# A transformer block with 32 experts on one core: the experts' weights through one ring of five buffers, eight units in the early sweep, and the end in quarters

## What is computed

```python
ada = silu(c) @ w_ada + b_ada                 # six vectors of 2048
h = rms_norm(x, g_pre_mix) * (1 + sc_m) + sh_m
y = token_mixer(h, ...)                       # h @ w_in (2048 x 6160), attention beside a gated scan, @ w_out
x = x + gt_m * rms_norm(y, g_post_mix)
h = rms_norm(x, g_pre_ffn) * (1 + sc_f) + sh_f
y = hier_moe(h, ...)                          # 32 experts, each row goes to two of one group
x = x + gt_f * rms_norm(y, g_post_ffn)
# an expert: (silu(t @ w1) * (t @ w3) * weight) @ w2, with w1, w3: 2048 x 512 and w2: 512 x 2048
```

## Time and profile before

| | us |
|---|---|
| median of 3 runs | 1546.67 (1545.41 to 1547.28) |
| the profiled execution, its own time | 1547.03 |
| its span, first to last instruction | 1545.2 |
| PE matmuls busy | 1168.6 (76%) |
| DVE busy | 717.6 (46%) |
| HBM read | 579.28 MB, 376 GB/s over the span |
| chain that ended last | PE 46%, DMA 35%, DVE 8% |

### The profile page before, as it was taken

The page is one execution under the profiler, slowest core; times in us unless marked ns, Lnnn a source line. Parts: engine busy times, 40 slices in busy tenths (PEclk is TensorE's granted clock), DMA queues, the critical chain, the costliest instruction groups (busy, mean ns, idle before and its releaser), DMA issues.

```text
span 1545.2 us, 21972 instructions
## 1 busy us (share of the span) xinstructions
PE 1168.6 (76%) x9147; PEld 602.4 (39%) x9148; DVE 717.6 (46%) x939; ACT 168.8 (11%) x432; POOL 41.1 (3%) x69
## 2 busy tenths in 40 slices
PE   5679999999999998757647646656655679699554
PEld 4568644754444454323223223222322334344221
DVE  5773256777484635422422422432332345446326
ACT  3001131221111020000000000000000000001001
POOL 0002000000000001000000000000000000000001
PEclk9789999999999997978877877887887889899877
DMA  9999877778788788999999999999999998999994
GB/s 360 395 401 358 318 301 300 299 274 342 269 306 332 300 331 339 429 426 425 434 424 425 432 426 425 434 423 425 431 426 425 431 427 372 387 389 391 427 426 180
DMA packets 93822, 581.83 MB, mean 377 GB/s; under 512 B 5752, under 2 KB 16272, under 8 KB 55904
## 3 DMA queue, kind: packets, MB, share of 16 engines
q1 hardware_dynamic: 91056, 571.49, 90.8%
q10 hardware_dynamic: 1520, 7.76, 1.2%
q0 software_dynamic: 1216, 2.17, 0.5%
HBM read 579.28 MB, written 2.13 MB: 376 GB/s over the span
## 4 chain that ended last, share of the span: by engine, by line
PE 46%; DMA 35%; DVE 8%; issue 5%; SPq 4%; ACT 1%; POOL 0%; DVEq 0%; ACTq 0%
DMA stream<-in_w 32%; PE ps L803 12%; PE ps L638 11%; PE ps L722 7%; PE ps L829 5%; DMA stream<-in_w_ada 3%; PE ps L555 3%; PE ps L635 3%; SPq L435 3%; PE ps L773 2%; DVE wk L1201 1%; DVE wk L876 1%; DVE wk L1195 1%; SPq L495 1%; DVE stream L925 1%
## 5 line engine op out<-in xcount | busy, mean ns | idle before, releaser
L803 PE MATMUL ps<-stream,wk 128*32 128x256 f32 x4608 | 310.4, 437 | 271.3 <-DMA stream<-in_w 269.8
L1153 DVE TENSOR_TENSOR acc<-ps,acc 128x2048 f32<-128x2048 f32 x37 | 84.8, 2292 | 576.7 <-PE ps L773 576.7
L803 PEld LDWEIGHTS ps<-stream,wk 128*32 128x32 f32 x4608 | 177.9, 126 | 417.1 <-issue 349.7
L638 PE MATMUL ps<-stream 128*128 128x512 f32 x448 | 197.3, 595 | 0.0
L829 PE MATMUL ps<-stream,wk 128*32 128x512 f32 x1152 | 131.2, 595 | 18.0 <-DVE wk L1205 18.0
L638 PEld LDWEIGHTS ps<-stream 128*128 128x128 f32 x448 | 83.5, 191 | 98.9 <-issue 98.8
L722 PE MATMUL ps<-stream 128*128 128x512 f32 x256 | 112.3, 601 | 3.1 <-ACT stream L1384 1.8
L555 PE MATMUL ps<-stream 128*128 128x256 f32 x448 | 107.0, 404 | 1.8 <-ACT stream L1280 1.8
L555 PEld LDWEIGHTS ps<-stream 128*128 128x128 f32 x448 | 91.3, 205 | 15.6 <-issue 1.9
L773 PE MATMUL ps<-wk,cst 32*128 32x512 f32 x592 | 84.1, 639 | 11.1 <-DVE acc L1153 10.1
L876 DVE SCALAR_TENSOR_TENSOR wk<-stream,cc,wk 128x1024 f32<-128x1024 f32 (+1 forms) x75 | 80.4, 1072 | 13.1 <-DMA stream<-in_w_ada 9.5
(11 more groups left out here) (247 smaller groups left out, 825.0 us busy)
## 6 DMA issues: line engine op xcount, KB each, us to landing
stream<-in_w SPq DMA_DIRECT2D x128, 2048.0 KB, 24.6
stream<-in_w SPq DMA_DIRECT2D x32, 4096.0 KB, 32.4
stream<-in_w_ada SPq DMA_DIRECT2D x64, 1024.0 KB, 5.6
stream<-in_w_ada SPq DMA_DIRECT2D x64, 512.0 KB, 11.7
stream<-in_w_in SPq DMA_DIRECT2D x8, 4096.0 KB, 16.7
stream<-in_w_out SPq DMA_DIRECT2D x4, 4096.0 KB, 15.8
stream<-in_w_in SPq DMA_DIRECT2D x3, 3584.0 KB, 18.9
stream<-in_w_in SPq DMA_DIRECT2D x2, 1792.0 KB, 10.7
```

The lines of the kernel that those rows point to most:

```text
L638: last = nc.tensor.matmul(bank(fill % 2), hT[:, k, P * half:P * half + P], w[:, k, :], start=(k == 0), stop=(k == KD - 1))
L803: last = nc.tensor.matmul(bank(1)[32 * g:32 * g + 32, 0:256], xe[:, k, :], a13[g // 2][:, k, 256 * (g % 2):256 * (g % 2) + 256], start=(k ...
L1153: V.tensor_tensor(y4, ps[:, b0:b0 + 4, :], y4, ALU.add).then_inc(ysum_sb, 1)
```

## The change

The three kinds of expert weights go through one ring. Load n (3e for w1 of expert e, 3e+1 for w3, 3e+2 for w2) uses buffer n mod 5, each in two halves with semaphores of their own. SyncE waits for the use of load n-5, which is w3 of e-2, w2 of e-2 or w1 of e-1: so w1 of e waits for the first product of expert e-2, w3 of e for the second product of e-2, w2 of e for the first product of e-1. PE's loop does five experts in a pass, and the last two are written out behind it.

In the early sweep there are eight units of 256 columns. Six keep a bank; units 6 and 7 take turns in one bank, and DVE adds their part of each stage to SBUF (`added`), in the midst of the next stage's pieces. PE takes the units in the order 6, 0, 1, 2, 7, 3, 4, 5. The half unit and its two slots are gone: 32 slots, attention from slot 6.

At the end PE puts the second half's earlier sum into PSUM with an identity product and adds the last part on top, DVE multiplies that with the gain straight from PSUM, ScalarE makes the roots, and both halves are finished and sent in four quarters each.

```diff
+RING = 5
-HEADS_READY = [10, 12]
+HEADS_READY = [8, 10]
-EARLY = 7
-SLOTS = 34
-ATT_FROM = 7
+EARLY = 8
+HELD = 6
+TURN = [6, 0, 1, 2, 7, 3, 4, 5]
+SLOTS = 32
+FILLS = HELD + SLOTS // 2
+ATT_FROM = 6
+ADA_AT = [0, 11, 21, SLOTS, SLOTS + 6]
...
-        early_w = [slab(s4, 4096, 2, 1792), slab(s3, 0, 4, 1792), slab(S2, 0, 4, 1792), slab(s3, 0, 4, 1792), slab(S2, 4096, 2, 1792)]
+        early_w = [slab(S2, 0, 2, 2048), slab(s3, 0, 4, 2048), slab(S2, 0, 4, 2048), slab(s3, 0, 4, 2048), slab(S2, 4096, 2, 2048)]
-        W1 = [stream[:, 0, :], stream[:, 1, :]]
-        W3 = [stream[:, 2, :], stream[:, 3, :]]
-        W2v = stream[:, 4, :].rearrange("p (k n) -> p k n", k=4)
+        def ring(n):
+            return stream[:, (0, 2, 4, 1, 3)[n % RING], :]
@@ SyncE
-                if j >= 3:
+                if j >= 2:
                     sp.wait_ge(stage_ps, j - 1)
                 sp.dma_start(early_w[j], w_in[:, lo:hi, 0:256 * EARLY]).then_inc(early_w_in[j], 16)
-            sp.dma_start(half_w, w_in[:, :, 256 * EARLY:2048]).then_inc(half_in, 16)
...
-            def load_w1(e, b):
+            def load_w1(e, r):
                 done = sp.value_load(cums[0:1, bass.ds(e - 1, 1)], min_val=1, max_val=MAX_TILES)
                 sp.wait_ge(ab_ps, done)
-                sp.dma_start(W1[b], w_unit(e, w1)).then_inc(w1_in[b], 16)
-            def load_w3(e, b):
                 for j in range(2):
-                    sp.dma_start(half(W3[b], j), half(w_unit(e, w3), j)).then_inc(w3_in[b][j], 16)
-            def load_w2(e):
+                    sp.dma_start(half(ring(r), j), half(w_unit(e, w1), j)).then_inc(ring_in[r % RING][j], 16)
+            def load_w3(e, r):
+                done = sp.value_load(cums[0:1, bass.ds(e - 1, 1)], min_val=1, max_val=MAX_TILES)
+                sp.wait_ge(ye_ps, done)
+                for j in range(2):
+                    sp.dma_start(half(ring(r), j), half(w_unit(e, w3), j)).then_inc(ring_in[r % RING][j], 16)
+            def load_w2(e, r):
                 done = sp.value_load(cums[0:1, bass.ds(e, 1)], min_val=1, max_val=MAX_TILES)
-                sp.wait_ge(ye_ps, done)
+                sp.wait_ge(ab_ps, done)
...
-            with sp.Fori(2, NE // 2) as i:
-                for b in range(2):
-                    load_w1(2 * i + b, b)
-                    load_w3(2 * i + b, b)
-                    load_w2(2 * i + b)
+            with sp.Fori(1, NE // RING) as i:
+                for b in range(RING):
+                    load_w1(RING * i + b, 3 * b)
+                    load_w3(RING * i + b, 3 * b + 1)
+                    load_w2(RING * i + b, 3 * b + 2)
@@ PE
             def early_unit(j, u):
                 lo, hi = STAGES[j]
+                held = u < HELD
+                if not held and j + u > HELD:
+                    pe.wait_ge(add_sb, 2 * j + u - HELD)
...
-            with pe.Fori(0, NE // 2) as i:
-                for b in range(2):
+            with pe.Fori(0, NE // RING) as i:
+                for b in range(RING):
+                    expert(i, b)
+            for b in range(NE % RING):
+                expert(NE // RING, b)
...
+            def earlier_sum(g):
+                nc.tensor.matmul(ps[:, g, :], ident, ysum[1][:, 512 * g:512 * g + 512], start=True, stop=False)
+            earlier_sum(0)
+            pe.wait_ge(ye_sb, total + 1)
             add_part(0, 4)
-            add_part(1, 0)
+            for g in range(1, 4):
+                earlier_sum(g)
+            add_part(1, 0, True)
@@ DVE
+            def added(j, u):
+                home = kaT[:, 2 * u - 8:2 * u - 6, :]
+                n = 2 * j + u - HELD
+                dve.wait_ge(add_ps, n + 1)
+                if j == 0:
+                    V.tensor_copy(home, bank(HELD, 2, S)).then_inc(add_sb, 1)
+                else:
+                    dve.wait_ge(add_sb, n)
+                    V.tensor_tensor(home, bank(HELD, 2, S), home, ALU.add).then_inc(add_sb, 1)
...
+                    if j and n_ in (len(pieces(j)) // 4, 3 * len(pieces(j)) // 4):
+                        added(j - 1, HELD + n_ // (len(pieces(j)) // 2))
...
             collect(0, 4)
+            link(V.tensor_tensor(fin_gained(0), ysum[0], g2b, ALU.mult))
-            collect(1, 0)
+            for j in range(2):
+                V.tensor_tensor(fin_gained(1)[:, 1024 * j:1024 * j + 1024]..., ps[:, 2 * j:2 * j + 2, :],
+                                g2b[:, 1024 * j:1024 * j + 1024]..., ALU.mult).then_inc(gain_sb, 1)
@@ ScalarE
-            for t in range(TT):
-                act.wait_ge(fin_sb, t + 1)
-                act.dma_start(out_d[:, t, :], fin_gained(t)).then_inc(fin_out, 16)
+            for t in range(TT):
+                for q in range(4):
+                    act.wait_ge(fin_sb, 4 * t + q + 1)
+                    act.dma_start(out_d[:, t, 512 * q:512 * q + 512], fin_gained(t)[:, 512 * q:512 * q + 512]).then_inc(fin_out, 16)
```

More of the change, by code:

```diff
@@ L124, in schedule @@
     beside = [[] for _ in range(SLOTS)]
[L125 to L129, removed]
+    beside[0].append(("alpha", 0))
+    beside[1].append(("row",))
+    beside[2] += [("alpha", 1), ("lam",)]
+    beside[4].append(("alpha", 2))
+    beside[5].append(("flip",))
     for m in (2, 3):
@@ L162, in loads @@
 def loads():
-    out = [(4 * i + 5.9, ("unit", i + 2)) for i in range(8)] + [(SLOTS + 2 * i + 1.9, ("unit", i + 10)) for i in range(2)]
+    out = [(4 * i + 3.9, ("unit", i + 2)) for i in range(8)] + [(SLOTS + 2 * i + 1.9, ("unit", i + 10)) for i in range(2)]
     out += [(max(ada_slot(n - 4) + 0.5, 1.9), ("ada", n)) for n in range(4, 64)]
@@ L550, in early_unit @@
                 lo, hi = STAGES[j]
+                held = u < HELD
+                if not held and j + u > HELD:
+                    pe.wait_ge(add_sb, 2 * j + u - HELD)
                 for part in range(2):
                     for k in range(lo, hi):
-                        if u == 0 and part == 0:
+                        if u == TURN[0] and part == 0:
                             pe.wait_ge(hT_act, k + 1)
-                        last = nc.tensor.matmul(bank(u, 2, S)[:, part, :], early_w[j][:, k - lo, 256 * u + P * part:256 * u + P * part + P], hT[:, k, :],
-                                                start=(k == 0 and part == 0), stop=(k == KD - 1 and part == 1))
+                        last = nc.tensor.matmul(bank(u if held else HELD, 2, S)[:, part, :], early_w[j][:, k - lo, 256 * u + P * part:256 * u + P * part + P], hT[:, k, :],
+                                                start=(k == (0 if held else lo) and part == 0), stop=(k == (KD if held else hi) - 1 and part == 1))
+                if not held:
+                    last.then_inc(add_ps, 1)
                 return last
@@ L579, in mod_sums @@
                 return last
-            fill = EARLY
+            fill = HELD
             for item in SCHED:
@@ L768, in pick_rows, with add_part @@
                 last.then_inc(rows_ps, 1)
-            def add_part(t2, b0):
+            def add_part(t2, b0, onto=False):
                 for g in range(4):
-                    last = nc.tensor.matmul(ps[:, b0 + g, :], spread[32 * g:32 * g + 32, t2, :], ye[32 * g:32 * g + 32, :], start=True, stop=True)
+                    last = nc.tensor.matmul(ps[:, b0 + g, :], spread[32 * g:32 * g + 32, t2, :], ye[32 * g:32 * g + 32, :], start=not onto, stop=True)
                 last.then_inc(part_ps, 1)
@@ L868, in early @@
                 out_ = early_acc[:, :, P * lo:P * hi]
-                for c, k0, k1 in pieces(j):
+                for n_, (c, k0, k1) in enumerate(pieces(j)):
                     dve.wait_ge(piece_in[c % 8], 32 * (c // 8 + 1))
@@ L910, in _ @@
                 early(j)
+            for u in range(HELD, EARLY):
+                added(len(STAGES) - 1, u)
             def accumulate(n):
```

283 lines of the change are left out of this document (151 added, 132 removed).

## The result

The changed kernel takes **1537.68 us** (median of 4 runs, 1536.35 to 1538.39) where the kernel before took 1546.97 beside it (1545.41 to 1548.34). The ratio is 0.994, with a 95% interval of 0.9926 to 0.9954: faster by 9.3 us. The prediction had 1524.7 us, with bounds that it works out as 1518.6 and 1533.8, so its direction was right and its size was not: it had named a gain of 22.3 us. The profiled span fell from 1545.2 to 1534.5 us.

The account below looks back on a forecast made before the run. The prediction took PE work to bound the first third and the weights' bytes the expert part. Savings of 15.6 (experts), 3.7 (sweep) and 3.0 (end), together 22.3, from 1547.03 gave 1524.7 us; range 1518.6 to 1533.8.

Parts of the forecast that it names:

- the experts' sum of -15.6 us: Expert part: the ring removes 14.3 us lost at two pairs and 1.3 us of emptiness at the start.
- their fetch: Rival, expert loop: five bodies do not stay resident and each expert's code is fetched again, 1567 us; chance 3%.
- Sweep: Early sweep: an eighth unit replaces two later slots; 3.3 + 1.5 + 5.6 - 14.05 = -3.7 us.
- term (1): Early sweep: 1.31 MB more goes ahead of stage 3's last modulation piece, costing +3.3 us.
- term (3): Early sweep: 24 records of the new unit fall into PE-bound work at 0.2335 us each, costing +5.6 us.
- the rival in which PE and DVE wait for each other: Early stages give back their gain, with a doubled attention stall: sweep +2 instead of -3.7, 1530 us; chance 12%.
- Start of the experts: Loads of the first experts: the ring issues w2 of expert 1 earlier, removing 1.3 us of emptiness.
- Experts 3 to 23: Steady expert stretch: the bytes stay the same, at 29.44 us an expert, so no change.
- The two pairs: Experts 23, 24, 26 and 27 with two tiles of rows: the ring loses nothing there, saving 14.3 us.
- slack of 5.6 us: At the pairs: the buffer comes free 5.6 us before the load needs it, some 1.3 us going to starting a transfer.
- End: Kernel's end: -1.2 us of DVE work and -1.8 for a smaller last transfer, -3.0 us; bounds -1 and -4.5.
- The third, the blocks: Sign against the forecast: a fetch row of more than some 60 blocks with PE idle beside landed weights.

Follow-up runs that it names:

- ten halves: The changed kernel's sweep and end, PE loop of three experts with two written out ahead, ten half buffers in a fixed table of places; 1526.68 us.
- loop of eight: The kernel before with only PE's expert loop written out eight times instead of two; 1563.34 us against 1547.87.
- loop of two: The changed kernel with PE's loop of two experts, w1 loaded whole and fixed uses for the ten half buffers; 1533.57 us.
- loop of four: The kernel before with only PE's expert loop written out four times instead of two; 1556.91 us, ratio 1.0065.
- ring alone: The kernel before with the change's ring and loop of five experts, without its sweep and end; 1543.24 us, ratio 0.9976.
- nine halves with two experts ahead: The changed kernel with a ring of nine half buffers, experts 0 and 1 written out ahead of a loop of three; 1531.52 us.
- w1 in halves: The kernel before with each w1 loaded as two halves in rows of 16 KB; 1550.48 us, ratio 1.0018.
- kernel without the ring: The changed kernel with its sweep and end, but experts, buffers and PE's loop of two as before; 1542.34 us, ratio 0.9968.

## Why the prediction was wrong

**The failed step is the experts' sum of -15.6 us** (measured, by the terms below, -1.9), and in it the price of code, which was put at nothing. The prediction took 29.44 us an expert as fixed by the bytes and asked of the loop of five only whether PE stalls longer than its 10.3 to 11.1 us of waiting. It saw that no row told whether five bodies stay resident, and put 3% on their fetch; for stalls at the five jumps back alone it took nothing. What happened is neither of the cases it priced. The bodies are fetched again in every expert (40 blocks in twenty experts, 2 x 16 KB for a body of some 26 KB), PE has its waits for weights to hide it in, and the *load queue* pays: 7.5 us over twenty experts after the short rows are taken out (597.9 less 590.4 of the ten halves), 0.19 us a block, beside 0.17 and 0.16 in the two kernels with written-out loops, with 36 and 19 blocks.

These prices are averages, and the cost is not spread evenly. Fifteen of the change's twenty experts take 29.40 to 29.72 us with 1 to 3 blocks each; the other five take 30.83 to 30.98 with 2 or 3 blocks, and they hold 7 of the 7.5 us. In the loop of eight, eight of the twenty take 30.1 to 30.2 us and the others 29.4 to 29.6.

In the case where fetching was priced as slower than before, PE had to stall. The trace of the change has a stop of 5.80 us before expert 25, where the loop jumps back, with one block on its way in it; it lies behind the twenty quiet experts in which the 7.5 us were lost. The stops before experts 2 and 29 (2.86 and 3.25 us) have no block in them, and the loop of two waits 2.81 us before expert 2 for its weights, so these two are not shown to be fetches.

That the blocks are the cause is shown: with them and without the ring it is slower, with the ring and without them it is fast. The loop of four shows it within one run. How one block of 16 KB delays the weights by 0.16 to 0.19 us, when 16 KB at 427 GB/s are 0.04 us, is argued, with three readings for it. The argument: a block occupies one of the 16 DMA engines, that engine falls behind the others, and PE waits for the part of a load that it carries. First, q8's 0.4% of 16 engines over 860 us is 1.0 us of one engine's time a block. Second, twenty experts need 251.7 MB, and the kernels without blocks move 251.5 to 251.7 MB between the starts of experts 3 and 23; the change moves 253.2 and the ring alone 253.3, the loops of eight and four 252.8 and 252.2. So 1.6 MB more had come in, worth 3.7 us, while the load that PE needed was not complete. Third, when the queue runs low at the pairs, the DMA share falls to nothing within 3 us in the kernel before (0.77, 0.19, 0.04, 0.00 in the windows of 1 us from 1283), and in the change it is 0.81, 0.57 and 0.54 in the three from 1279 and 0.85, 0.62 and 0.38 in the three from 1312, when SyncE's next load is issued: some engines have work left when others have none. No experiment here was made on it, and why some blocks cost nothing stays open.

Term by term, by the table (spans; forecast, measured):

- *Sweep:* -3.7, measured **-5.3** in this execution. The fold of stage 3 was worked out to come at 120.5 and came at 120.60, but that is luck. DVE's new wait was put at nothing, and 1.98 of its 26.9 us lie on the path to this fold; the late start of the pieces, term (1), was 2.1 us in place of 3.3 (96.26 against 94.12), the two additions took 1.2 in place of 1.5, and the 14 pieces 0.4 less than before. In the nine halves with two experts ahead the same wait is 0.54 us, and the fold comes 1.4 us earlier, at 119.21. From fold to fold PE's loop took 33.45 us, where 32.4 were worked out. The error that shows in the sum is in term (3): the 224 records behind the fold take 50.75 us to the first slot, 0.227 each, where 0.2335 were used. So the rival in which PE and DVE wait for each other had its mechanism right, at 2 us once, and not its sum.
- *Start of the experts:* -1.3, measured **-0.3**. The hole in the queue is filled (423 GB/s from 615 to 620, where 313 were), but PE's wait before expert 2 only fell from 3.37 to 2.86 us. It is 2.87 in the ten halves and 2.81 in the loop of two. What sets it is not shown.
- *Experts 3 to 23:* 0, measured **+9.1**: 1.5 for rows of 16 KB (from w1 in halves: 0.074 x 20) and 7.5 for blocks. Here the forecast fails.
- *The two pairs:* -14.3, measured **-10.7**. The difference of 3.6 is as large as 8 x 0.45 us of the slower pace. But the reasoning with a slack of 5.6 us did not hold as written: the queue ran low ahead of w2's issues at 1281.69, 1314.66 and 1405.98, the first of which, behind expert 23, the prediction had not looked at. What this cost by itself is not shown: the queue was never wholly empty, the 1.6 MB that had come in ahead were used up in this stretch (99.3 MB moved where eight experts need 100.7), and expert 29 starts 179.5 us after expert 23, six times the pace again. The run with ten halves has nearly the full size, -13.5, with a table made to give the loads at the pairs their place earlier. Whether five whole buffers would do it without blocks no run shows. The nine halves show the price of a ring that is too short: 6.5 us more than with ten.
- *End:* -3.0, measured **-3.4**.

The sum is -10.6 against a measured span of -10.7. The early stages did not give back their gain. Of what the prediction said would show it wrong, two came: windows under 400 GB/s at the pairs (283 to 341), and DVE's new wait in the early stages, 26.9 us where more than 3 was the sign. The second was a poor sign, as most of that wait cost nothing. The third, the blocks, came at 55 in the window, below the 60 that it had named and with PE mostly waiting for weights rather than beside them: the sign that mattered was set too high.

The rule that the prediction set against the change, from the Trainium skill, Runtime: NRT & Kernel Launch, Instruction fetch mechanics, gives PE 128 KiB, and lets a jump stall when its target is outside "the current 2-page window", with pages of 16 KiB. The prediction read the whole buffer as that window, and the runs bear it out in so far as two bodies (53 KB by the prediction's estimate) and three (80 KB) jump back without a block. They agree that a limit exists but not quite with its place: four bodies (107 KB) stay at times and are fetched again at others, and of five everything is. Stops where the loop jumps back, as it warns of, are seen at the pairs (5.80 us in the change, 3.12 to 3.53 in the written-out loops); the price that the loads pay is not in it. Where the Trainium skill and a run differ, the run decides.

The second lesson is in the maps. The kernel with ten halves reaches 1526.7 us, 2 us above the forecast, and its span is 20.8 us shorter than that of the kernel before: -5.2 to expert 0, -0.2 to expert 3, +1.6 for short rows, -13.5 at the pairs, -3.5 at the end. The forecast came near to what a ring of this size can be worth, and was wrong about this way of writing it.

## What to carry to other kernels

Count the code of a loop that is to be written out more often as memory traffic of its own: look for the engine's instruction queue in a window of the steady part, and if it is not empty where every queue is full of loads, each block costs the loads, on the average, more than its bytes say. If a rotation needs a long period, look for a shorter one over smaller places before unrolling; the last waits that matter are few, and a fixed table can give just those the early place. And when a stretch is "bound by bytes", its pace is still a term of the sum and not a constant: row length and foreign packets both moved it here.

## What the runs showed of the hardware

- PE's instruction memory kept loops of two and three bodies (0 and 3 blocks between 640 and 1500 us) and not those of five and eight (55 and 52 blocks). Four bodies it kept for stretches only (31 blocks, none from 1026 to 1273 us).
- A 16 KB block beside a full load queue cost 0.16 to 0.19 us of the loads' time on the average of twenty experts, in four kernels; the cost came in steps of 0.6 us (loop of eight) and 1.4 us (the change), in some experts and not in others.
- The DMA engines of one queue can get out of step: with blocks among the loads the DMA share sank over three us to 0.38 when the queue ran low (to 0.00 in the kernel before), and 1.6 MB of later loads were in before the one that PE waited for.
- Loads in rows of 16 KB instead of 32 KB for a third of the bytes moved the pace from 29.44 to 29.51 us an expert.
- The same code can meet another clock. After a wait of 1.57 us the change did 16 matmuls at the full clock, and the kernel without the ring did them 1.7 us slower:

```profile
367.54 7.03 PE L651 MATMUL ps<-stream 128*128 128x512 f32 x16
```
```profile
368.40 8.71 PE L641 MATMUL ps<-stream 128*128 128x512 f32 x16
```

The granted clock of the 11 us around it was 1.00 (all at 2.4 GHz) in the one and 0.84 in the other (in part at 1.2 GHz). From 275 to 298 us, behind a wait of 3.35 and 3.36 us, it was 1.00 and 0.85, and that cost 2.9 us. With DVE's wait in the sweep (0.54 to 1.98 us) such things spread the start of expert 0 over 5.5 us in six kernels with the same work up to there. Differences of one to three us ahead of the experts in a single profiled execution are therefore no evidence about a part; the totals above rest on medians of 4 to 10 runs.
